# Two column halves for shift and scale at the start of a two-block transformer kernel, and half of three weight chunks ahead of the second

## The chip, the cores and the metric

The kernel runs on one core of one Trainium2 chip. The metric is the time of one execution on the device, in microseconds (us): the median of the runs. In the rows PE is TensorE (matrix multiply; PEld its weight load), DVE is VectorE, ACT is ScalarE, POOL is GpSimd, and SP only issues DMAs.

## What is computed

Two transformer blocks work on 256 tokens of width 2048, all in float32. The change is in the start of the first, up to its first output projection:

```python
silu_c = jax.nn.silu(c)
mod = silu_c @ w_ada[l] + b_ada[l]                    # w_ada: 2048 x 12288
shift_m, scale_m, gate_m, shift_f, scale_f, gate_f = jnp.split(mod, N_MOD, axis=-1)
h = modulate(rmsnorm(x, g_norm_mix[l]), shift_m, scale_m)   # normed * (1 + scale) + shift
proj = h @ w_in[l]                                    # w_in: 2048 x 3904
dq, dk, dv, q_lat, kv_lat, k_pe = jnp.split(proj, IN_SPLITS, axis=-1)
...                                                   # differential attention on dq, dk, dv
q = (rmsnorm(q_lat, g_q_a[l]) @ w_q_b[l]); kv = (rmsnorm(kv_lat, g_kv_a[l]) @ w_kv_b[l])
...                                                   # latent attention (MLA) on q, kv, k_pe
x = x + gate_m[:, None, :] * (jnp.concatenate([o_diff, o_mla], axis=-1) @ w_out[l])
```

`c` is one vector, so each of the six parts of `mod` is a vector of 2048. The rest of the first block (a 8192 wide feed-forward with its own shift, scale and gate) and the whole second block stay as they are.

## The kernel before

**Every weight passes a ring of four slots** (`RING`, `w_raw`), 1 MiB each. SP issues a load (line 399) when the slot's last user has released it. There are two kinds of load. A *weight load* holds four contraction tiles of 128 rows by 512 columns; ACT rounds it in two *halves* of 1024 columns to `w_hi` (L424), DVE subtracts to get `w_lo` (L429), and PE multiplies each half with 12 matmuls of 512 columns (L470: h_hi with w_hi, h_hi with w_lo, h_lo with w_hi; two contraction tiles, two token tiles). `w_hi` and `w_lo` also have four slots, one per half, so ACT can be at most four halves ahead of PE. A *chunk* is 512 output columns; with 16 contraction tiles it has 8 halves, and goes to one of two PSUM accumulators, `acc`.

An *ada load* holds 128 rows of one of the six parts of `w_ada`, 128x2048. DVE multiplies it with one value of silu(c) per row and adds it to `acc_ada` (L1575 for the first of 16, L1578 for the others; called a MAC below). After 16 of them the sum over the 128 partitions is taken by 16 matmuls against a column of ones (L2636, L2645 for the first scale; `ada_sum`) or, for a gate that is wanted in every row, by 4 matmuls of 512 columns (L2848, `gate_sum`), which ACT copies out (L1028).

**The start.** SP issues four ada loads, then x, then the other 28 of shift and scale. The parts come in the order `ADA_ORDER`: shift, scale, shift of the feed-forward, `gate_m`, scale of the feed-forward, last gate. When DVE has done all 32 MACs, PE sums the scale, DVE makes the factors (L1613, L1615), and piece by piece (two tiles of h of eight) ACT scales the transposed x (L772), DVE rounds (L1662) and subtracts (L1663), and PE starts on chunk 0.

**The chunks** of `w_in`, `w_q_b` and `w_kv_b` stand in `FIRST`, numbered 0 to 14. Halves are numbered through by g: chunk n of `w_in` has the halves 8n to 8n+7, g = 64 to 69 are `w_q_b`, 70 to 73 `w_kv_b`. `FIRST_MACS` says after which loads of a chunk an ada load follows. Everything else is hung on g by hand in `first_step`: copies of finished chunks (L884, L1803), rotary parts (L1766 to L1771), transposes (L494), latent norms. `HEAD_AT` says at which g each of the eight heads of the differential attention starts; a head is scores (L2771), a maximum (L1849), exponentials on ACT, the difference of the two softmaxes (L1861), a transpose, and the values (L2758). Heads 0 to 3 are normed by `head_scaled(0)` (L1838, L1841).

**After g = 73** come the transposes for the latent attention, and a loop over its eight heads (scores L2857 and L2858, maximum L1967, norm L1960, values L2876, copy L1973), with one MAC per turn on DVE (turn i is head i). In turns 0 and 1 PE and ACT also do the four gate sums. Then the output projection `w_out` starts: 4 chunks of 8 halves, 2 MACs each.

Engines run their own instructions in the order of the program and wait on semaphores; nothing is reordered.

## Time and profile before

| | us |
|---|---|
| median of 3 runs | 2719.41 |
| lowest and highest | 2716.62, 2720.58 |
| profiled execution | 2724.19 |
| its span, first to last instruction | 2722.5 |
| start of chunk 0 / 3 / 7 on PE in that span | 102.3 / 177.5 / 286.1 |
| start of `w_out` on PE | 415.8 |

A row of a timeline gives the start, the length, the engine and the line of an instruction; "x3" joins three in a row, and brackets tell how long the engine had been idle and what released it. The chain is the work that ended last, followed back from the end; each piece waited for the piece before it. Rows by stretch give busy time per engine, TensorE's granted clock (1.00 is full), and the share of their time in which the 16 DMA engines were busy, with what they moved.

### The profile page before, as it was taken

The page shows a single profiled execution, that of the slowest core. Times are in us where ns is not written, and L with a number is a line of the kernel's source. Part 1 is how long each engine was busy: PE and PEld are TensorE (multiplying, and loading weights), DVE is VectorE, ACT ScalarE, POOL GpSimd, SP SyncE. Part 2 cuts the span into 40 slices and gives each one's busy share as a digit, 9 for nine tenths or more (in the row PEclk, how much of TensorE's full clock was granted, in tenths as well). Part 3 has the DMA queues.
Part 4 walks back from the last instruction along what each step waited for, and adds up shares of the span by engine and source line. Part 5 has one row for each costly group of instructions (what it writes and reads, how often), then busy time and mean ns, then how long its engine had stood idle before and what let it go on. Part 6 is the DMA issues. An engine that isn't in the chain of part 4 may idle for free.

```text
span 2722.5 us, 30665 instructions
## 1 busy us (share of the span) xinstructions
PE 2594.5 (95%) x11981; PEld 2149.9 (79%) x11981; DVE 1637.6 (60%) x1806; ACT 1212.7 (45%) x1631; POOL 10.8 (0%) x62
## 2 busy tenths in 40 slices
PE   1699879999999999999999999999999999999999
PEld 1577767788888888888888888888888888888887
DVE  7888677777455555556555775556555554454554
ACT  1346444544433444444444664454444343344343
POOL 0000000000000000000000000000000000000000
PEclk9999899999999999999999999999999999999999
DMA  9898457687555556555554584345555555555554
GB/s 399 304 356 312 166 199 284 225 288 277 201 187 187 190 186 208 188 183 194 188 167 162 175 262 140 124 155 186 185 185 183 197 189 187 196 187 191 189 194 139
DMA packets 254815, 566.08 MB, mean 208 GB/s; under 512 B 9967, under 2 KB 25068, under 8 KB 242156
## 3 DMA queue, kind: packets, MB, share of 16 engines
q1 hardware_dynamic: 252164, 562.87, 60.1%
q10 hardware_dynamic: 2538, 1.65, 0.2%
q8 instruction: 77, 1.26, 0.2%
q14 instruction: 36, 0.29, 0.0%
HBM read 562.39 MB, written 2.10 MB: 207 GB/s over the span
## 4 chain that ended last, share of the span: by engine, by line
PE 88%; DVE 7%; DMA 3%; issue 1%; ACT 1%; ACTq 0%; DVEq 0%
PE acc L470 81%; DVE acc_ada L1578 3%; PE tp L494 3%; DVE w_lo L429 2%; DMA w_raw<-in_w_ada_dram 1%; DMA w_raw<-in_w_in_dram 1%; PE sc L3035 1%; PE sc L3127 0%; PE sc L3126 0%; ACT w_hi L424 0%; PE sc L3143 0%; PE sc L2645 0%; PE tp L2758 0%; DMA rowsA<-in_g_norm_mix_dram 0%; PE tp L2848 0%
## 5 line engine op out<-in xcount | busy, mean ns | idle before, releaser
L429 DVE TENSOR_TENSOR w_lo<-w_raw,w_hi 128x1024 fp32r<-128x1024 f32 (+2 forms) x878 | 1053.7, 1217 | 580.0 <-ACT w_hi L424 572.0
L424 ACT ACTIVATE w_hi<-w_raw 128x1024 fp32r<-128x1024 f32 (+2 forms) x878 | 913.0, 1055 | 868.9 <-PE acc L470 782.1
L470 PE MATMUL acc<-w_hi,h_hi 128*128 128x512 f32 (+2 forms) x2272 | 715.1, 396 | 5.2 <-DVE w_lo L429 4.0
L470 PE MATMUL acc<-w_lo,h_hi 128*128 128x512 f32 (+2 forms) x2272 | 701.5, 390 | 0.0
L470 PE MATMUL acc<-w_hi,h_lo 128*128 128x512 f32 (+2 forms) x2272 | 700.1, 389 | 0.0
L470 PEld LDWEIGHTS acc<-w_lo,h_hi 128*128 128x128 f32 x2272 | 428.9, 189 | 89.3
L470 PEld LDWEIGHTS acc<-w_hi,h_lo 128*128 128x128 f32 x2272 | 428.4, 189 | 89.0
L470 PEld LDWEIGHTS acc<-w_hi,h_hi 128*128 128x128 f32 x2272 | 418.5, 190 | 88.8 <-issue 7.5
L470 PE MATMUL acc<-w_hi,f_hi 128*128 128x512 f32 x864 | 268.7, 392 | 0.0
L470 PE MATMUL acc<-w_lo,f_hi 128*128 128x512 f32 x864 | 266.3, 389 | 0.0
L470 PE MATMUL acc<-w_hi,f_lo 128*128 128x512 f32 x864 | 265.9, 389 | 0.0
L1578 DVE SCALAR_TENSOR_TENSOR acc_ada<-w_raw,cT,acc_ada 128x2048 f32<-128x2048 f32 x92 | 216.0, 2348 | 12.0 <-DMA w_raw<-in_w_ada_dram 8.5
L470 PEld LDWEIGHTS acc<-w_lo,f_hi 128*128 128x128 f32 x864 | 162.2, 188 | 34.0
L470 PEld LDWEIGHTS acc<-w_hi,f_lo 128*128 128x128 f32 x864 | 162.2, 188 | 33.8
L470 PEld LDWEIGHTS acc<-w_hi,f_hi 128*128 128x128 f32 x864 | 161.5, 188 | 34.5 <-issue 1.2
L2017 DVE TENSOR_TENSOR relu<-relu 128x1024 f32<-128x1024 f32 x16 | 19.6, 1226 | 51.6 <-ACT relu L1076 51.6
L1076 ACT ACTIVATE relu<-acc 128x1024 f32<-128x1024 f32 x16 | 16.4, 1028 | 71.4 <-PE acc L470 71.4
L1748 DVE SCALAR_TENSOR_TENSOR h_lo<-tp,vecB,h_hi 128x256 fp32r<-128x256 f32 x32 | 14.0, 480 | 53.0 <-ACT h_hi L848 53.0
L2593 DVE SCALAR_TENSOR_TENSOR hs<-acc,stat,sg 128x512 f32<-128x512 f32 x22 | 15.5, 746 | 48.1 <-ACT sg L1492 48.1
L729 ACT ACTIVATE sc<-x_residual 128x512 f32<-128x512 f32 x40 | 23.6, 591 | 46.4 <-DVE x_residual L1995 21.0
L2569 DVE TENSOR_TENSOR f_lo<-tp,f_hi 128x512 f32 (+1 forms) x22 | 14.2, 686 | 48.5 <-ACT f_hi L1502 48.5
L494 PE MATMUL tp<-ident,rowsB 65*128 65x65 f32 x1 | 0.4, 370 | 44.8 <-DMA perow<-in_cmp_pe_v_dram 44.8
(425 smaller groups left out, 1688.9 us busy)
## 6 DMA issues: line engine op xcount, KB each, us to landing
w_raw<-in_w_ff_dram SPq DMA_DIRECT2D x128, 1024.0 KB, 5.3
w_raw<-in_w_in_dram SPq DMA_DIRECT2D x108, 1024.0 KB, 5.0
w_raw<-in_w_ada_dram SPq DMA_DIRECT2D x96, 1024.0 KB, 6.4
w_raw<-in_w_ffn_gate_dram SPq DMA_DIRECT2D x44, 1024.0 KB, 5.0
w_raw<-in_w_ffn_up_dram SPq DMA_DIRECT2D x44, 1024.0 KB, 5.0
w_raw<-in_w_ffn_down_dram SPq DMA_DIRECT2D x44, 1024.0 KB, 5.0
w_raw<-in_w_out_dram SPq DMA_DIRECT2D x32, 1024.0 KB, 5.0
w_raw<-in_w_up_fox_dram SPq DMA_DIRECT2D x8, 1024.0 KB, 5.0
```

Source lines behind the costliest of these rows:

```text
L424: nc.scalar.activation(dst, src, ACT.Copy).then_inc(hi_done, 1)
L429: nc.vector.tensor_tensor(dst, src, hi.bitcast(F32), ALU.subtract).then_inc(lo_done, 1)
L470: last = nc.tensor.matmul(acc[b][:, t, 0:width], st[:, kt, t * P:(t + 1) * P], w[:, slot, kt - 2 * j, 0:width], start=(kt == 0 and n == 0) ...
L494: last = nc.tensor.transpose(tp[b][dst], src, ident[0:k, 0:k])
L729: last = nc.scalar.activation(sc[t][:], x[:, t, c * CW:(c + 1) * CW], ACT.Square, accum_out=sums[:, k:k + 1])
L1076: nc.scalar.activation(relu[:], acc[a.slot(2)][:], ACT.Relu).then_inc(acc_free[a.slot(2)], 2)
L1578: V.scalar_tensor_tensor(a[:], w, c_k, a[:], ALU.mult, ALU.add).then_inc(S("mac_done"), 1)
L1748: last = V.scalar_tensor_tensor(h_lo[:, k, :], tp[u.slot(2)][:, kk * T:(kk + 1) * T], vecB[:, gain0 + k:gain0 + k + 1], h_hi[:, k, :].bitc ...
L2017: V.tensor_tensor(relu[:], relu[:], relu[:], ALU.mult).then_inc(S("relu_squared"), 1)
L2569: V.tensor_tensor(f2_lo[:, cols, :], tp[u.slot(2)][:].rearrange("p (a b) -> p a b", a=2), f2_hi[:, cols, :].bitcast(F32), ALU.subtract).th ...
L2593: V.scalar_tensor_tensor(hs2[:, t, :], acc[a.slot(2)][:, t, :], stat[:, 6 + t:7 + t], sg2[:, t, :], ALU.mult, ALU.mult).then_inc(acc_free[ ...
L3035: last = MM(dst, st, wk, start=q in (0, 6) and j == 0 and k == 0 and m == 0, stop=q in (5, 9) and j == 1 and k == 3 and m == 1)
```

## The change

- **Halves of columns.** Shift and scale are made in two stages of 1024 columns. An ada load now holds 1024 columns of shift and the same 1024 of scale for 128 rows, 128x2x1024 in rows of 4 KB in place of 8 KB. Stage 0 gives the first 8 tiles of h, stage 1 the last 8. x is loaded before all of them.
- **Rows on PE.** Five of the 16 loads of stage 0 (`ROW_TILES`) are multiplied on PE, 4 matmuls of 512 columns each with one column of silu(c) as the weights; the result is one row, which DVE adds to partition 0 (`row_sums`).
- **Half of the contraction ahead.** After stage 0 the first two loads of each of the chunks 0, 1, 2 go through, between the ada loads of stage 1 (`FRONT_W`, `FRONT_MACS`); then the last two of each. Chunk 2 goes to the two `sc` banks, since `acc` holds only two chunks.
- **MACs later.** The first three chunks lose their 10 MACs of later parts. Chunk 6 gets 4 (was 2), chunk 7 gets 3 (was 1), the attention loop 10 (was 8), each `w_out` chunk 3 (was 2). The four gate sums move from turns 0 and 1 of the attention loop to behind it.
- **Moved by hand:** heads 0 to 3 from g = 30, 33, 36, 39 to 36, 39, 42, 45; rotary parts of chunks 0 and 1 from g = 16, 22 to 26, 28, and their four transposes from 18, 19, 24, 25 to 28 to 31; the ones-sum of part 2 from g = 54 to 62; `head_scaled(0)` from 57 to 69; `mod_column(3)` from 57 to 66. The latent heads' outputs go to a buffer of their own (`oM`). `row_sums`, `front_mods` and so on are new functions for the start.

```diff
-FIRST_MACS = ((0, 2), (0, 1, 2, 3), (0, 1, 2, 3), (0, 1, 2, 3), (0, 1, 2, 3), (0, 1, 2, 3), (0, 2), (1,)) + 7 * ((0,),)
+FIRST_MACS = ((), (), (), (0, 1, 2, 3), (0, 1, 2, 3), (0, 1, 2, 3), (0, 1, 2, 3), (0, 1, 3)) + 7 * ((0,),)
 FIRST_TILES = {"w_in": KD, "w_q_b": 4, "w_kv_b": 2}
-HEAD_AT = (30, 33, 36, 39, 53, 56, 59, 62)
+FRONT_CHUNKS, STAGES = 3, 2
+ROW_TILES = (1, 4, 7, 10, 13)
+FRONT_W = ((0, 0), (0, 1), (1, 0), (1, 1), (2, 0), (2, 1), (0, 2), (0, 3), (1, 2), (1, 3), (2, 2), (2, 3))
+FRONT_MACS = ((0,), (1, 2, 3), (4, 5), (6, 7, 8), (9, 10, 11, 12, 13, 14), (15,))
+HEAD_AT = (36, 39, 42, 45, 53, 56, 59, 62)
...
+        mix_acc = place("mix_acc", [P, STAGES, D], F32, 0)
...
+        oM = place("oM", [P, HEADS, T], F32, 66)
...
+        front_load, at = {}, 0
+        for k in range(KD):
+            front_load["ada", 0, k] = at
+            at += 1
+        for i, piece in enumerate(FRONT_W):
+            front_load[piece] = at
+            at += 1
+            for k in FRONT_MACS[i] if i < len(FRONT_MACS) else ():
+                front_load["ada", 1, k] = at
+                at += 1
+
+        def mac_count(s, k):
+
+            return KD + k + 1 if s else k + 1 - sum(1 for r in ROW_TILES if r <= k)
...
-            ada_loads(RING)
             sp.dma_start(x[:], A["x"][0].rearrange("(t p) d -> p t d", p=P)).then_inc(S("x_loaded"), 16)
-            ada_loads(2 * KD - RING)
-            for nth in range(len(FIRST)):
-                if nth == 1:
+            for what, L in front_load.items():
+                if what[0] == "ada":
+                    _, s, k = what
+                    src = A["w_ada"][0][k * P:(k + 1) * P, 0:2 * D].rearrange("p (g n) -> p g n", g=2)
+                    freed = (S("row_macs"), ROW_TILES.index(k) + 1) if s == 0 and k in ROW_TILES else (mac_done, mac_count(s, k))
+                    ring(At(L), raw[:, At(L).slot(RING)].rearrange("p (g a) n -> p g (a n)", g=2),
+                         src[:, :, s * D // 2:(s + 1) * D // 2], freed[0], At(freed[1]))
+                else:
+                    nth, q = what
+                    name, col, width, nk = first_part(nth)
+                    src = A[name][0][CW * q:CW * (q + 1), col:col + width].rearrange("(k p) n -> p k n", p=P)
+                    ring(At(L), raw[:, At(L).slot(RING)], src, lo_done, At(2 * FRONT_W.index(what) + 2))
...
-            ada_loads(HEADS)
-            weights(A["w_out"][0], 4, KD, macs=2)
+            ada_loads(HEADS + 2)
+            weights(A["w_out"][0], 4, KD, macs=3, uniform=0)
...
+            front_hi(0, 0)
+            front_hi(0, 1)
+            for p in range(4):
+                front_piece(p)
+            for nth, q in FRONT_W[2:7]:
+                front_hi(nth, q)
+            front_piece(4)
+            front_piece(5)
+            front_hi(0, 3)
+            front_piece(6)
+            front_piece(7)
+            for nth, q in FRONT_W[8:]:
+                front_hi(nth, q)
...
-                if i < 2:
-                    for q in (2 * i, 2 * i + 1):
-                        gate_rows(gate_m, q)
-                    if i == 1:
-                        use += 4
-                if i >= 1:
...
+            for q in range(4):
+                gate_rows(gate_m, q)
+            use += 4
...
+            def row_sums():
+
+                dve.wait_ge(S("row_macs"), len(ROW_TILES))
+                dve.wait_ge(S("mac_done"), mac_count(0, KD - 1))
+                for c in range(4):
+                    to = mix_acc[0:1, 0, c * CW:(c + 1) * CW]
+                    last = V.tensor_tensor(to, to, acc[c // 2][0:1, c % 2, :], ALU.add)
+                last.then_inc(S("mac_done"), len(ROW_TILES))
...
+            row_sums()
+            front_lo(0, 0)
+            front_mac(1, 0)
+            front_mods(0)
+            front_lo(0, 1)
+            front_piece(0)
+            front_piece(1)
+            front_mac(1, 1)
+            front_mac(1, 2)
+            front_piece(2)
+            front_mac(1, 3)
+            front_piece(3)
+            for i in range(2, 6):
+                front_lo(*FRONT_W[i])
+                for k in FRONT_MACS[i]:
+                    front_mac(1, k)
+            front_lo(0, 2)
+            positions()
+            angles(0)
+            angles(1)
+            dve.sem_inc(S("angles_reduced"), 1)
+            front_mods(1)
+            front_piece(4)
+            front_piece(5)
+            front_lo(0, 3)
+            front_piece(6)
+            front_piece(7)
+            for nth, q in FRONT_W[8:]:
+                front_lo(nth, q)
...
-                    one_mac()
+                one_mac()
...
-            ada_sum(0, 2)
...
+            pe.wait_ge(S("mac_done"), 1)
+            for nth, k in enumerate(ROW_TILES):
+                L = At(front_load["ada", 0, k])
+                pe.wait_ge(raw_loaded[L.slot(RING)], L.round(RING).times(16).val(16))
+                for c in range(4):
+                    last = MM(acc[c // 2][0:1, c % 2, :], cT[:, k:k + 1], raw[:, L.slot(RING), c, :], start=nth == 0,
+                              stop=nth == len(ROW_TILES) - 1)
+                last.then_inc(S("row_macs"), 1)
...
+            front_turns(0)
+            for i, (nth, q) in enumerate(FRONT_W):
+                if i == 5:
+                    front_turns(1)
+                width = first_part(nth)[2]
+                for jj in range(2):
+                    j = 2 * q + jj
+                    pe.wait_ge(S("mix_ready"), j + 1)
+                    pe_half(pe, At(2 * i + jj), nth % 2, j, KD, width, h_hi, h_lo,
+                            [sc[t][:, 0:width] for t in range(NT)] if nth == FRONT_CHUNKS - 1 else None)
+                    if i in (0, 6):
+                        front_turn(j + 2)
+            pe.wait_ge(S("small_loaded"), 16 * SMALL)
+            TR(pe, At(11), [((slice(0, P), slice(0, NROWS)), rowsB[0:NROWS, :])])
+            use = 12
...
-                if i < 2:
-                    for q in (2 * i, 2 * i + 1):
-                        gate_sum(GATE_M, use, q)
-                    if i == 1:
-                        use += 4
...
+            for q in range(4):
+                gate_sum(GATE_M, use, q)
+            use += 4
```

DVE at the start of the program, before. `acc_ada` is where the MACs add, `w_lo` a weight half, `h_lo` a piece of h, `xs` the normed x:

```order
3 L1575 TENSOR_SCALAR acc_ada<-w_raw,cT 128x2048
4 L1578 SCALAR_TENSOR_TENSOR acc_ada<-w_raw,cT,acc_ada 128x2048 x15
5 L1575 TENSOR_SCALAR acc_ada<-w_raw,cT 128x2048
6 L1578 SCALAR_TENSOR_TENSOR acc_ada<-w_raw,cT,acc_ada 128x2048 x3
...
15 L1578 SCALAR_TENSOR_TENSOR acc_ada<-w_raw,cT,acc_ada 128x2048
16 L1592 TENSOR_TENSOR modT<-tp,vecA 128x16
17 L1578 SCALAR_TENSOR_TENSOR acc_ada<-w_raw,cT,acc_ada 128x2048 x8
18 L1613 TENSOR_TENSOR modT<-sc,vecA 128x4
19 L1615 SCALAR_TENSOR_TENSOR gmod<-modT,vecA 128x4
20 L429 TENSOR_TENSOR w_lo<-w_raw,w_hi 128x1024
```

And now, from the last MACs of stage 0 to the factors of stage 1 (`mix_acc` takes the place of `acc_ada`):

```order
9 L1679 SCALAR_TENSOR_TENSOR mix_acc<-w_raw,cT,mix_acc 128x2048 x4
10 L1687 TENSOR_TENSOR mix_acc<-mix_acc,acc 1x512 x4
11 L460 TENSOR_TENSOR w_lo<-w_raw,w_hi 128x1024 x2
12 L1676 TENSOR_SCALAR mix_acc<-w_raw,cT 128x2048
13 L1702 TENSOR_TENSOR modT<-tp,vecA 128x8
...
26 L460 TENSOR_TENSOR w_lo<-w_raw,w_hi 128x1024 x2
27 L1679 SCALAR_TENSOR_TENSOR mix_acc<-w_raw,cT,mix_acc 128x2048 x6
28 L460 TENSOR_TENSOR w_lo<-w_raw,w_hi 128x1024 x2
29 L1679 SCALAR_TENSOR_TENSOR mix_acc<-w_raw,cT,mix_acc 128x2048
30 L460 TENSOR_TENSOR w_lo<-w_raw,w_hi 128x1024 x2
31 L1748 CAST pos_f<-pos_i 128x2
```

Six weight loads now stand among the 16 MACs of stage 1, and the rotary angles (from row 31) stand ahead of the factors of stage 1 (row 48).

ACT at the end of the latent attention, before (`pmT` are transposed probabilities, `h_hi` rounded attention outputs, L424 the first halves of `w_out`):

```order
180 L1035 ACTIVATE pm,sums<-acc,mxs 128x256 x2
181 L1048 ACTIVATE pmT<-tp 128x512 x2
182 L424 ACTIVATE w_hi<-w_raw 128x1024 x2
183 L780 ACTIVATE h_hi<-oT 128x512
```

and now:

```order
179 L1107 ACTIVATE pm,sums<-acc,mxs 128x256 x2
180 L1115 ACTIVATE pmT<-tp 128x512 x2
181 L1100 ACTIVATE gate_m<-tp 128x512 x4
182 L455 ACTIVATE w_hi<-w_raw 128x1024 x2
183 L801 ACTIVATE h_hi<-oM 128x512
```

The four copies of the gate sums stand directly ahead of the first weight halves of `w_out`.

## Rows read from the trace of the kernel before

**Rows 1.** The page: busy time by engine; the chain by engine.
```profile
PE 2594.5 (95%) x11981; PEld 2149.9 (79%) x11981; DVE 1637.6 (60%) x1806; ACT 1212.7 (45%) x1631; POOL 10.8 (0%) x62
...
PE 88%; DVE 7%; DMA 3%; issue 1%; ACT 1%; ACTq 0%; DVEq 0%
```

**Rows 2.** Busy time by stretch; DMA share and GB/s stand last.
```profile
core 0: us, PE busy (x) PEld busy (x) DVE busy (x) ACT busy (x) POOL busy (x), PEclk, DMA share, GB/s
20.00:40.00 20.00, 0.00 (x0) 0.00 (x0) 15.96 (x7) 6.62 (x17) 0.00 (x0) 1.00 1.02 420
...
1200.00:1500.00 300.00, 299.08 (x1393) 249.00 (x1392) 167.91 (x211) 135.19 (x178) 0.00 (x0) 1.00 0.54 180
177.50:286.00 108.50, 107.66 (x529) 87.29 (x529) 89.48 (x107) 58.30 (x115) 0.00 (x0) 0.98 0.84 300
...
311.00:375.00 64.00, 47.19 (x225) 38.04 (x224) 46.07 (x65) 29.03 (x63) 0.00 (x0) 0.84 0.52 192
```

**Rows 3.** Timeline of DVE up to chunk 0: start, us, instruction, idle before.
```profile
22.64 2.35 DVE L1578 SCALAR_TENSOR_TENSOR acc_ada<-w_raw,cT,acc_ada 128x2048 f32<-128x2048 f32 x1 [5.06 <-DMA w_raw<-in_w_ada_dram]
...
46.19 7.26 DVE L1578 SCALAR_TENSOR_TENSOR acc_ada<-w_raw,cT,acc_ada 128x2048 f32<-128x2048 f32 x3 [0.37 <-DMA w_raw<-in_w_ada_dram]
53.47 1.28 DVE L1575 TENSOR_SCALAR acc_ada<-w_raw,cT 128x2048 f32<-128x2048 f32 x1
...
75.90 19.54 DVE L1578 SCALAR_TENSOR_TENSOR acc_ada<-w_raw,cT,acc_ada 128x2048 f32<-128x2048 f32 x8 [0.65 <-DVE modT L1592]
97.40 0.16 DVE L1613 TENSOR_TENSOR modT<-sc,vecA 128x4 f32<-128x4 f32 x1 [1.96 <-PE sc L2645]
...
99.51 0.69 DVE L1663 TENSOR_TENSOR h_lo<-ttmp,h_hi 128x512 fp32r<-128x512 f32 x1
...
105.82 2.34 DVE L429 TENSOR_TENSOR w_lo<-w_raw,w_hi 128x1024 fp32r<-128x1024 f32 x2
```

**Rows 4.** The chain at the start: start, us, engine and line.
```profile
51.10 2.35 DVE acc_ada L1578
...
95.49 6.99 PE sc L2645 x32
102.48 5.33 PE acc L470 x12
...
108.33 2.79 PE acc L470 x12
```

**Rows 5.** Timeline of ACT: one piece scaled, one weight half rounded.
```profile
97.85 1.02 ACT L772 ACTIVATE ttmp<-tp,modT,gmod 128x256 f32<-128x256 f32 x2 [1.34 <-DVEq L1617]
98.76 1.05 ACT L424 ACTIVATE w_hi<-w_raw 128x1024 fp32r<-128x1024 f32 x1
```

**Rows 6.** The gate sums' line on PE: ns min/median/max (two records each matmul).
```profile
L2848 PE MATMUL tp<-acc_ada,ones x16: 590/592/594, 376.1 to 725.0; 128*128 128x512 f32 x16
```

**Rows 7.** The loads' line on SP, first 120 us: issue to landing.
```profile
DMA to landing us min/median/max: 5.0/7.4/12.6
```

**Rows 8.** Timeline of PE: transposes after a pause; first matmuls of chunks 2, 3.
```profile
75.45 1.09 PE L494 MATMUL tp<-ident,xs 128*128 128x128 f32 x4 [4.67 <-DVEq L1593]
...
154.72 0.62 PE L470 MATMUL acc<-w_hi,h_hi 128*128 128x512 f32 x2
...
177.53 0.70 PE L470 MATMUL acc<-w_hi,h_hi 128*128 128x512 f32 x2
```

**Rows 9.** The chain between chunk 7 and the latent attention.
```profile
347.57 0.69 DVE proj L1803
348.26 2.26 DVE acc_ada L1578
...
353.09 2.18 issue
```

**Rows 10.** Timeline of DVE: heads 4 to 7 normed; the third maximum of the loop.
```profile
361.58 1.29 DVE L1841 TENSOR_TENSOR proj<-proj,rcp 128x512 f32<-128x512 f32 x2
...
384.50 0.69 DVE L1967 TENSOR_REDUCE mxs<-acc 128x2 f32<-128x512 f32 x1 [1.10 <-PE acc L2858]
```

**Rows 11.** The chain at the end of the latent attention.
```profile
376.25 1.72 PE tp L2848 x4
...
409.88 0.63 DVE pm L1960 x2
410.55 0.66 PE tp L494 x4
411.20 2.88 PE sc L2876 x8
414.14 0.30 issue
414.44 1.23 DVE w_lo L429
415.81 9.25 PE acc L470 x27
```

**Rows 12.** Timeline of ACT: two of the four copies of the gate sums.
```profile
377.93 1.08 ACT L1028 ACTIVATE gate_m<-tp 128x512 f32<-128x512 f32 x2
```

400 lines of the change are left out of this document (216 added, 184 removed).

## The prediction

> **What bounds the kernel now.** First the page: TensorE is busy for 95% of the span, and the chain lies on it for 88% [rows 1]. So nearly everywhere only less work for TensorE would shorten the kernel, and the change takes no matmul away; it can gain only where TensorE stands idle. The stretches show where. From 20 to 40 us it does nothing at all, while DMA is full (share 1.02) [rows 2]; DVE's timeline and the chain go on like that to 95.5 us, first MACs that wait for loads, then MACs back to back [rows 3, 4]. The second idle place is between chunk 7 and the output projection: 47.2 us busy of 64 from 311 to 375 [rows 2]. In between (177.5 to 286.0, chunks 3 to 6) TensorE is busy 107.7 of 108.5 us, DVE 89.5, DMA 84% [rows 2].
>
> I take the working in two parts: when chunk 3 starts (before: 177.5 [rows 8]), and what the way from there to `w_out` costs more or less. Behind that, TensorE has work without gaps; a third MAC per `w_out` chunk adds 2.4 us of DVE to chunks of 22 us in which DVE has some 7 us to spare, and I count it at nothing; if that room were gone, it would cost 2.4 us for each of 4 chunks.
>
> **Stage 0.** Before, the 16th MAC begins at 51.10 and ends at 53.5 [rows 4], behind x and 16 loads; nine loads took 46.19 - 22.64, 2.62 us each, with DMA full [rows 3, 2]. The new order brings the same bytes, so 53.5 is where I start. Two things delay it.
> The rows are now 4 KB long. No row shows that. With rows of 8 KB the stretch gives 420/1.02 = 412 GB/s of a full DMA share, with the 2 KB rows of the feed-forward weights 180/0.54 = 333 [rows 2]: 2.55 and 3.15 us for 1 MiB. If a DMA row has a fixed cost, 4 KB lies a third of the way up: 2.75, or 16 x 0.20 = 3.2 us (ends 0 and 9.6).
> The five loads on PE: a 512 column float32 matmul takes 1.72/2 = 0.86 us [rows 11], two records each [rows 6]. After a pause TensorE works at 1.2 GHz: the sums take 6.99 us and the first half 5.33 against 2.79 later [rows 4], four transposes 1.09 after 4.67 us of pause [rows 8]. So a load takes 3.4 to 6.9 us there, where a MAC takes 2.4. At the longer time the slot comes free so late that, with 5.0 us from issue to landing [rows 7], DMA idles 1.4 us (6.9 + 5.0 against four loads of 2.62); five times gives 0 to 7. The engine gets warm during such a row, so I take 0.8 in all. The last MAC of stage 0 then ends at 53.5 + 3.2 + 0.8 = 57.5.
> The rule of the Trainium skill that speaks against my 3.2 is in "DMA: Bandwidth & Descriptors", Specifications: line rate needs at least 512 B. By it 4 KB would cost nothing over 8 KB, and both stages would end earlier, the sum by about 4 us. The trace does not bear it out as it stands, since the 2 KB stretch gives 333 and not 412 GB/s for a full share.
>
> **Stage 1.** From 57.5 the path is: four additions of one row, 2.6 (the nearest row is an h_lo of 512 columns, 0.69 with 0.1 overlapped [rows 3]); 16 sums by TensorE out of a pause, 7.0 [rows 4]; the factors, three operations as L1613 at 0.16 with gaps [rows 3], 0.8. That is 68.0. From here DVE has a list without a hole: w_lo of the second load 2.3, four pieces 2.6, 15 MACs at 19.54/8 = 2.44 make 36.7, w_lo of four loads 9.3 (2.34 each) [rows 3], together 50.9. It also waits: for the first pieces (ACT 1.02 and about 0.6 more) [rows 5], and for w_hi halves that ACT can't make until TensorE has freed a slot. 2.5 us, ends 0 and 6. The last MAC ends at 121.4. DMA by itself: 22 loads, 16 x 2.75 + 6 x 3.15 = 62.9 behind 55.1, plus the MAC: 120.4. Two engines are thus equally late here, and neither can be speeded up alone. TensorE meanwhile does ten halves, 28 us at full clock, 53 at half, in 51: it comes through, warm or in part cold.
> At 121.4 the sums again find TensorE out of a pause (it had nothing since the fifth weight load): 7.2. The rotary angles on DVE (4.6) lie beside them. Factors 0.8, a transpose that needs the bank they free 1.1, and TensorE starts the 11th half at 130.8, the first at low clock. 14 halves at 2.74 ((177.53 - 154.72 - 0.9)/8 [rows 8]) make 38.4, the low clock 2.5 (5.33 - 2.79), two transposes 1.0: **chunk 3 starts at 172.7**, 4.8 us earlier than 177.5. Its 33 us of matmuls ahead are worth so little since the last MAC, which ended at 95.5, now ends at 121.4, and is followed by 14 halves instead of 24 with their own MACs between.
>
> **From chunk 3 to w_out.** (a) Two transposes that stood in chunk 2 come into chunk 3: +0.9. (b) In chunks 3 to 6 DVE gets 2 more MACs (4.9), two rotary parts and lambda (4.3): 98.7 us of work in about 103 (the ones-sum has left for chunk 7), where it had 89.5 in 108.5 [rows 2]. Its lead of up to four halves hides most; +1.0, ends 0 and 4. (c) Chunk 7: the ones-sum comes in with its own cold matmuls behind it, which only moves 6 us; two more MACs, 4.9 us of DVE, of which the chunk has 7 us idle: +1.0, ends 0 and 4. (d) `head_scaled(0)`, 1.3 us for its two products [rows 10] and 0.4 of small ones, moves out of chunk 7 to g = 69, where the chain is DVE [rows 9]; with `mod_column` +1.9, ends 1 and 2.5. (e) The latent loop: without gate sums in the first two turns, the third maximum does not wait 1.10 us [rows 10], and the MAC that only writes (L1575, 1.28 [rows 3]) falls into a turn that DVE bounds: -1.9. At the end DVE's two extra MACs go into the pauses for the last values. But TensorE does four gate matmuls, 3.4 us or 6.9 cold [rows 11], and **ACT stands in order**: the last gate copy (0.54 [rows 12]) must be done before the first w_hi of `w_out` (1.05), then w_lo (1.2). From the end of the values, 414.1 - 1.9, that is 412.2 + 3.4 + 0.6 + 1.05 + 1.2 = 418.5, or 422.0 cold, where it was 415.8 [rows 11]: +2.7 to +6.2, I take +4.2. Before, the w_hi was made under the values.
> Sum: 0.9 + 1.0 + 1.0 + 1.9 + 4.2 = +9.0, against -4.8: **+4.2**. The profiled execution (2724.2, span 2722.5) would become 2728.4; it lies 4.8 above the median of the runs, so the median goes from 2719.4 to 2723.6. Differences under about 0.2% (5.4 us) can't be told from none in a measurement of this kernel.
>
> **Rivals.** (1) **Faster**: DMA takes 4 KB rows like 8 KB, no slot is held up, DVE waits for nothing. Stage 0 ends at 53.5, the last MAC at 53.5 + 10.5 + 50.9 = 114.9, chunk 3 starts at 166.2: -11.3. With (b), (c) at nothing, (d) 1, (e) 2.7: +4.6, together -6.7, 2713; with the sums at full clock too (3.5 twice) 2706. For it: DVE took its MACs without a hole from 75.9 to 95.4 [rows 3]. This takes in the skill's rule on row lengths. I name it 2711. (2) **Slower, the ring**: a weight load holds its slot until ACT and DVE are through with it, and ACT waits for TensorE's w_hi slots at low clock; so both bounds of stage 1 add up instead of lying beside each other. It decides as soon as the holes of stage 1 exceed 6 us: last MAC at 127, chunk 3 at 178.4, +0.9 + 9.0 = 2729. For it: issue to landing of 7.4 in the median [rows 7], nearly the whole turn of a ring of four. Against: in the same rows DVE kept 2.44 a load. (3) **Slower, the way behind**: the start gains 4.8, but (b), (c), (d) and (e) stand at their upper ends, 0.9 + 4 + 4 + 2.5 + 6.2 = 17.6: 2732. (4) That TensorE doesn't start ahead at all: only if the first pieces of h waited for stage 1, and the order of DVE's rows excludes it; no chance of its own.
>
> **Chances.** Forecast 0.36, from 2714 to 2724.8, within 0.2%; faster (1) 0.27; slower (2) 0.27 and (3) 0.10. So faster 0.27, same 0.36, slower 0.37. The signs are nearly balanced, since a gain of 5 to 11 stands against a loss of 5 to 12 at other places. The range takes in most of (1) and of (2) and (3): 2709 to 2732. The forecast's own range is 2716 to 2729.
>
> **What will show it.** Five groups of four row matmuls on TensorE, 3.4 to 6.9 us each; last MAC of stage 0 near 57.5, of stage 1 near 121; a pause of TensorE before each ones-sum and 7 us for each; chunk 3 at 172.7; between stage ends DMA share near 1; `w_out` starting 5 to 8 us behind the last values instead of 1.7. I am wrong if chunk 3 starts before 168 or after 177, or if ACT's gate copies end without TensorE waiting.

## The result and the profile after

| | before | after |
|---|---|---|
| median, us | 2719.41 | 2728.50 |
| lowest and highest | 2716.62, 2725.27 | 2723.52, 2735.17 |
| runs | 11 | 11 |
| profiled execution (span) | 2724.19 (2722.5) | 2728.53 (2726.6) |

The changed kernel is slower: ratio 1.0029, 95% interval 1.0021 to 1.0037, or 7.9 us (5.7 to 10.1). The range held it (2709 to 2732). The likeliest case, 2723.6 and within 0.2% of before, did not come: it was 0.29%, the slower side.

Again first the page of the changed kernel, the engines and the chain by engine; [rows 1] are the same lines of before.

```profile
PE 2625.1 (96%) x12021; PEld 2159.9 (79%) x12021; DVE 1620.8 (59%) x1794; ACT 1221.5 (45%) x1643; POOL 10.8 (0%) x62
...
PE 92%; DVE 4%; DMA 2%; ACT 1%; issue 1%; SPq 0%; DVEq 0%; ACTq 0%
```

TensorE is busy 31 us longer: the row matmuls (24.0 us in five groups), and more matmuls at low clock. By stretch, as [rows 2] (columns: busy us and instructions of PE, PEld, DVE, ACT, POOL, then the clock, DMA share, GB/s):

```profile
core 0: us, PE busy (x) PEld busy (x) DVE busy (x) ACT busy (x) POOL busy (x), PEclk, DMA share, GB/s
20.00:40.00 20.00, 9.13 (x18) 1.30 (x16) 9.01 (x7) 1.49 (x2) 0.00 (x0) 0.83 0.93 351
177.50:286.00 108.50, 108.20 (x546) 88.45 (x544) 97.94 (x126) 62.26 (x127) 0.00 (x0) 1.00 0.89 320
311.00:375.00 64.00, 45.11 (x217) 36.19 (x215) 44.82 (x66) 26.87 (x57) 0.00 (x0) 0.84 0.49 180
```

From 20 to 40 us the DMA share is 0.93, where it was 1.02: the loads no longer come without a gap. From 177.5 to 286 DVE is busy 97.9 us where it was 89.5, and from 311 to 375 TensorE does even less than before. DVE's timeline answers to [rows 3]; "x4" with L1687 is `row_sums`:

```profile
28.32 2.35 DVE L1679 SCALAR_TENSOR_TENSOR mix_acc<-w_raw,cT,mix_acc 128x2048 f32<-128x2048 f32 x1 [7.07 <-DMA w_raw<-in_w_ada_dram]
...
37.00 4.80 DVE L1679 SCALAR_TENSOR_TENSOR mix_acc<-w_raw,cT,mix_acc 128x2048 f32<-128x2048 f32 x2 [3.79 <-DMA w_raw<-in_w_ada_dram]
...
54.77 2.35 DVE L1679 SCALAR_TENSOR_TENSOR mix_acc<-w_raw,cT,mix_acc 128x2048 f32<-128x2048 f32 x1 [0.35 <-DMA w_raw<-in_w_ada_dram]
57.23 2.47 DVE L1687 TENSOR_TENSOR mix_acc<-mix_acc,acc 1x512 f32<-1x512 f32 x4
...
120.37 2.35 DVE L1679 SCALAR_TENSOR_TENSOR mix_acc<-w_raw,cT,mix_acc 128x2048 f32<-128x2048 f32 x1
```

The MACs wait 7.07 and 3.79 us for loads; the last of stage 0 ends at 57.1, the last of stage 1 at 122.7. The timeline of TensorE, as [rows 8], shows the same from the other side, and what follows:

```profile
33.87 5.08 PE L2839 MATMUL acc<-w_raw,cT 128*1 128x512 f32 x8 [8.54 <-DMA w_raw<-in_w_ada_dram]
...
59.75 6.99 PE L2851 MATMUL tp<-ones,mix_acc 128*128 128x1 f32 x32 [5.17 <-DVE mix_acc L1687]
...
122.86 6.96 PE L2851 MATMUL tp<-ones,mix_acc 128*128 128x1 f32 x32 [14.10 <-DVE mix_acc L1679]
...
173.28 1.06 PE L510 MATMUL acc<-w_hi,h_hi 128*128 128x512 f32 x2 [1.78 <-DVE w_lo L460]
...
335.55 2.05 PE L2902 MATMUL tp<-proj,pdT 128*128 128x128 f32 x8 [6.33 <-DVE c_lo L1946]
```

Both ones-sums stand behind a pause and take 7 us. Chunk 3 starts at 173.28, 4.2 us earlier than before. At 335.55 the values wait 6.33 us for the last `c_lo`. Before it was 4.90:

```profile
334.19 2.04 PE L2758 MATMUL tp<-proj,pdT 128*128 128x128 f32 x8 [4.90 <-DVE c_lo L1823]
```

The chain at the end of the latent attention, against [rows 11]:

```profile
410.48 1.82 PE sc L3013 x8
412.30 3.54 PE tp L2990 x8
...
416.36 1.06 ACT w_hi L455
417.44 1.24 DVE w_lo L460
418.81 21.34 PE acc L510 x86
```

`w_out` starts at 418.81 in place of 415.81. Behind that, hardly anything is left that the change made. The offset between the two traces is 1.72 us at the first gate product behind `w_out`, 2.79 at the first relu of the feed-forward part, the same 2.79 at the places behind it up to 1546 us, and 4.04 from 1668 us on. Each step is a stretch at low clock that is longer in one trace than in the other, with the same instructions and pauses. At the start of the feed-forward part before has

```profile
515.24 1.22 PE L470 MATMUL acc<-w_hi,h_hi 128*128 128x512 f32 x2
516.26 1.05 PE L470 MATMUL acc<-w_lo,h_hi 128*128 128x512 f32 x2
517.11 0.79 PE L470 MATMUL acc<-w_hi,h_lo 128*128 128x512 f32 x2
```

and after

```profile
516.97 1.22 PE L510 MATMUL acc<-w_hi,h_hi 128*128 128x512 f32 x2
...
520.55 1.05 PE L510 MATMUL acc<-w_lo,h_hi 128*128 128x512 f32 x2
521.40 0.71 PE L510 MATMUL acc<-w_hi,h_lo 128*128 128x512 f32 x2
```

A pair of records is 1.05 us at 1.2 GHz and 0.62 at 2.4. After has five pairs of the low kind (two of them stand in the gap) where before has two, though both began the same way.

### The profile page after: what moved, and what is told of

It reads as the page before. It is cut to its first block, busy times and chain, and to the rows that moved or that the text cites. A ratio compares the mean times of both kernels' runs of the same rounds, so it can differ in the third digit from the quotient of the medians.

```text
span 2726.6 us, 30768 instructions
## 1 busy us (share of the span) xinstructions
PE 2625.1 (96%) x12021; PEld 2159.9 (79%) x12021; DVE 1620.8 (59%) x1794; ACT 1221.5 (45%) x1643; POOL 10.8 (0%) x62
## 4 chain that ended last, share of the span: by engine, by line
PE 92%; DVE 4%; DMA 2%; ACT 1%; issue 1%; SPq 0%; DVEq 0%; ACTq 0%
PE acc L510 83%; PE tp L534 3%; DMA w_raw<-in_w_ada_dram 2%; DVE acc_ada L1648 1%; DVE w_lo L460 1%; DVE mix_acc L1679 1%; PE sc L3175 1%; PE sc L510 1%; DMA w_raw<-in_w_in_dram 1%; PE tp L2851 1%; PE sc L3267 0%; PE sc L3266 0%; PE sc L2917 0%; PE sc L3283 0%; PE tp L2902 0%
## 5 line engine op out<-in xcount | busy, mean ns | idle before, releaser
L510 PE MATMUL acc<-w_hi,h_hi 128*128 128x512 f32 (+2 forms) x2240 | 705.0, 396 | 8.1 <-DVE w_lo L460 5.9
L510 PE MATMUL acc<-w_lo,h_hi 128*128 128x512 f32 (+2 forms) x2240 | 691.9, 390 | 0.0
L510 PE MATMUL acc<-w_hi,h_lo 128*128 128x512 f32 (+2 forms) x2240 | 690.4, 390 | 0.0
L510 PEld LDWEIGHTS acc<-w_lo,h_hi 128*128 128x128 f32 x2240 | 423.4, 189 | 87.9
L510 PEld LDWEIGHTS acc<-w_hi,h_lo 128*128 128x128 f32 x2240 | 422.6, 189 | 87.5
L510 PEld LDWEIGHTS acc<-w_hi,h_hi 128*128 128x128 f32 x2240 | 413.0, 190 | 91.3 <-issue 11.8
L1648 DVE SCALAR_TENSOR_TENSOR acc_ada<-w_raw,cT,acc_ada 128x2048 f32<-128x2048 f32 x62 | 145.5, 2346 | 1.1 <-DVE proj L1991 1.1
L1679 DVE SCALAR_TENSOR_TENSOR mix_acc<-w_raw,cT,mix_acc 128x2048 f32<-128x2048 f32 x25 | 58.8, 2350 | 21.6 <-DMA w_raw<-in_w_ada_dram 20.6
L2839 PE MATMUL acc<-w_raw,cT 128*1 128x512 f32 x40 | 24.0, 758 | 22.6 <-DMA w_raw<-in_w_ada_dram 22.6
```

The lines of the kernel that those rows point to most:

```text
L510: last = nc.tensor.matmul(banks[t], st[:, kt, t * P:(t + 1) * P], w[:, slot, kt - 2 * j, 0:width], start=(kt == 0 and n == 0), stop=(kt == ...
L1648: V.scalar_tensor_tensor(a[:], w, c_k, a[:], ALU.mult, ALU.add).then_inc(S("mac_done"), 1)
L1679: V.scalar_tensor_tensor(to, w, cT[:, k:k + 1], to, ALU.mult, ALU.add).then_inc(S("mac_done"), 1)
L2839: last = MM(acc[c // 2][0:1, c % 2, :], cT[:, k:k + 1], raw[:, L.slot(RING), c, :], start=nth == 0, stop=nth == len(ROW_TILES) - 1)
```

## The experiments

All ratios are to the kernel before; times of starts are from one profiled execution of each.

**The kernels once more.** Nothing is edited here; these two were run again for their traces.

> The kernel before, unchanged, profiled a second time. Theory (how fast the first loads land differs from execution to execution, with all behind it fixed): the 16th MAC ends 0.5 to 2.5 us off 53.45 and chunk 3 starts off 177.53 by less, and TensorE's clock at the start of w_out and of the feed-forward part rises at another instant, with up to 3 us in it. Rival (the first profile is exact): every start within 0.3 us.

Ratio 0.9999 (0.9990 to 1.0009), and yet a span of 2714.3 us in place of 2722.5. The 16th MAC ended at 54.1 instead of 53.5 and chunk 3 started at 178.0 (2.8 us ahead of its first transposes, as in the first trace) instead of 177.5. Then it got ahead:

```profile
411.24 0.70 PE L470 MATMUL acc<-w_hi,h_hi 128*128 128x512 f32 x2 [1.74 <-DVE w_lo L429]
```

`w_out` starts 4.6 us earlier than in the first trace. The row of the stretch from 280 to 430 us, first of the first trace, then of this one, says why:

```profile
280.00:430.00 150.00, 119.62 (x581) 97.12 (x581) 114.09 (x168) 68.03 (x154) 1.81 (x1) 0.87 0.55 196
```

```profile
280.00:430.00 150.00, 120.00 (x607) 97.45 (x608) 117.52 (x171) 71.21 (x156) 1.80 (x1) 0.93 0.59 209
```

120 us of TensorE at a mean clock of 0.87 lose 15.6 us to the low clock, at 0.93 only 8.4. (Busy time times what the clock lacks to 1.00.) The same product, added up in stretches of 10 us over the whole span, gives 21.4 us for the first trace and 12.9 for the second, and the spans are 8.2 us apart. The prediction had read its rows behind 286 us from an execution with more low clock. The theory is right in kind, but the effect is larger than it allowed: 4.6 us at `w_out`, not up to 3.

> The changed kernel, unchanged, profiled a second time. Theory (the rows of this kernel that repeat are fixed by its order, and the part that differs is the landing of the first loads and the instants at which TensorE's clock changes): the last MAC of stage 0 ends at 57 to 59.5, chunk 3 starts at 173 to 175.5, w_out 242 to 246 us behind it. Rival (the difference of 7.9 us is all order): chunk 3 and w_out start within 0.3 us of 173.28 and 418.81.

Ratio 1.0027 (1.0017 to 1.0037). The last MAC of stage 0 ended at 59.8, 2.7 us later than in the first trace, and

```profile
176.40 0.70 PE L510 MATMUL acc<-w_hi,h_hi 128*128 128x512 f32 x2 [1.78 <-DVE w_lo L460]
```

chunk 3 starts at 176.40 and `w_out` at 421.65, 245.3 us behind it (245.5 in the first trace). With the three variants below that keep this start there are five traces: chunk 3 at 173.3, 173.8, 175.0, 175.3, 176.4, on average 174.8. The first trace was the earliest of the five. The rival is out; the theory holds in kind, though 59.8 and 176.40 lie 0.3 and 0.9 us outside its limits.

**Rows on TensorE.** `ROW_TILES` empty, `row_sums` gone:

```diff
-ROW_TILES = (1, 4, 7, 10, 13)
+ROW_TILES = ()
...
-            row_sums()
```

> The changed kernel with all 16 loads of stage 0 as MACs on DVE, none as rows on TensorE, and so without the four additions of row_sums (2.47 us). Theory (stage 0 is bound by DMA, so the row matmuls take nothing off the path and only add row_sums): the last MAC of stage 0 ends within 0.8 us of 57.1, the ones-sum starts at 57.0 to 57.8 in place of 59.75, and chunk 3 starts 1 to 2.5 us earlier than 173.28. Rival A (DVE would be late with 16 MACs at 2.35 us): the last MAC ends at 58.5 or later, and nothing is won. Rival B (the row matmuls held ring slots and cost DMA time): the last MAC ends at 55.5 or earlier, the first MACs without pauses, and chunk 3 starts 3.5 us or more earlier.

Ratio 1.0016 (1.0007 to 1.0024), 3.5 us less than the changed kernel. Both ratios have intervals of about 2 us to either side, so a difference between two of them is known to about 3 us; that holds for each such difference below. The last MAC of stage 0:

```profile
50.63 4.84 DVE L1679 SCALAR_TENSOR_TENSOR mix_acc<-w_raw,cT,mix_acc 128x2048 f32<-128x2048 f32 x2 [0.16 <-DMA w_raw<-in_w_ada_dram]
...
55.62 6.96 PE L2850 MATMUL tp<-ones,mix_acc 128*128 128x1 f32 x32 [47.34 <-DVE mix_acc L1679]
```

The last MAC ends at 55.5, the ones-sum starts 4.1 us earlier, chunk 3 at 170.40, 2.9 earlier. My theory was wrong in its first half: the row matmuls did take something off the path. The DMA share from 20 to 30 us, first of the changed kernel, then of this one:

```profile
20.00:30.00 10.00, 4.05 (x10) 0.59 (x8) 2.94 (x2) 1.28 (x1) 0.00 (x0) 1.00 0.83 288
```

```profile
20.00:30.00 10.00, 0.00 (x0) 0.00 (x0) 7.33 (x6) 1.13 (x1) 0.00 (x0) 1.00 0.97 357
```

With rows 288 GB/s, without 357. The slot that is held can be followed: the MAC that waits 7.07 us at 28.32 is that of load 5, which goes to the slot of load 1, and load 1 was in the row matmuls of 13.98 to 20.46. Without rows its MAC ended at 16.28, and no MAC of the stage behind the first waits more than 1.4 us. Rival B is right in kind, though chunk 3 gained less than its 3.5 us; over all traces the last MAC of stage 0 ends at 57.1 to 59.8 with rows (five) and at 55.5 to 57.1 without (five), 2.2 us apart on average, and `row_sums` comes on top.

**Rows of 4 KB.** The kernel before with the shape of its first 32 loads changed:

```diff
-                src = A["w_ada"][0][bass.ds(k.times(P).val(), P), group * D:(group + 1) * D]
+                src = A["w_ada"][0][m.k % KD * P:(m.k % KD + 1) * P, 0:2 * D].rearrange("p (g n) -> p g n", g=2)
+                src = src[:, :, s * D // 2:(s + 1) * D // 2]
```

> The kernel before with only the shape of its first 32 loads changed: 128 rows of 2 x 1024 columns in pieces of 4 KB, where it had rows of 8 KB; order, bytes, MACs and everything else as before (the shift and scale are then made of other columns, so its values differ from the reference). Theory (4 KB pieces cost 0.2 us for each load of 1 MiB): the last MAC of the 32 ends 6.4 us (5 to 8) later than 95.5, chunk 0 starts near 108.7 in place of 102.3, and the time rises by 5 to 7.5 us. Rival (the length of the pieces does not matter from 512 B up): all of these within 1 us of before.

The last eight MACs begin at 80.63, before at 75.90 [rows 3], and chunk 3 4.8 us later:

```profile
80.63 19.54 DVE L1584 SCALAR_TENSOR_TENSOR acc_ada<-w_raw,cT,acc_ada 128x2048 f32<-128x2048 f32 x8 [0.64 <-DVE modT L1598]
...
182.28 0.70 PE L470 MATMUL acc<-w_hi,h_hi 128*128 128x512 f32 x2 [0.94 <-DVE w_lo L429]
```

The 16th MAC ended 3.1 us later (56.6), 0.5 of it since the first began later. So a load costs 0.13 to 0.19 us more; for 16 loads that is 2.6 to 3.1 us where the theory had 3.2, and for 32 it was 4.7 where it had 6.4, short of its range. The same share of DMA moved less, from 30 to 40 us 403 GB/s at 1.03 in this kernel against 422 at 1.02 in the kernel before. "DMA: Bandwidth & Descriptors" of the Trainium skill (Specifications) gives 512 B as the least transfer for line rate. This trace does not bear out that everything above is the same. But the ratio is 1.0003 (0.9995 to 1.0012), 0.8 us. `w_out` was 4.0 us later than in the first trace of before, and that although the low clock took less from 280 to 430 us:

```profile
280.00:430.00 150.00, 119.91 (x607) 97.87 (x604) 112.72 (x170) 71.81 (x164) 1.80 (x1) 0.91 0.55 191
```

That is 10.8 us by this row, against 15.6 and 8.4 in the two traces of before. The interval of the time ends at 3.3 us, below the 4.7. The clock was a little better than before in the mean of all executions, 0.9918 against 0.9911; over the 2594.5 us in which TensorE is busy that is 1.8 us, an estimate. How much of a delay of 4.7 us at the start is left at the end is not settled.

**Warm before the second ones-sum.** Ten unused matmuls at once, and the angles moved:

```diff
+                    for _ in range(10):
+                        MM(tp[b][:], ones[:], mix_acc[:, 0, 0:CW], start=True, stop=True)
                 pe.wait_ge(S("mac_done"), KD * (s + 1))
...
-            positions()
-            angles(0)
-            angles(1)
-            dve.sem_inc(S("angles_reduced"), 1)
             front_mods(1)
```

> The changed kernel with ten 512 column matmuls whose result is not used, on TensorE ahead of the second ones-sum (in its pause of 14.1 us), and with the rotary angles (4.6 us on DVE) moved from ahead of front_mods(1) to behind the last w_lo of the front. Theory (the second ones-sum pays the low clock, 6.96 us for 32 records): it takes 3.5 to 4 us, the half behind it starts at 127 to 128 in place of 131.31 and is at full clock, and chunk 3 starts 4 to 6 us earlier than 173.28. Rival A (what follows stage 1 is bound by loads or by ACT and DVE, not by TensorE): the sum is shorter but chunk 3 moves by less than 2 us. Rival B (the extra matmuls run at the low clock throughout and end behind the last MAC): the sum starts later than 122.86 and nothing is won.

Ratio 1.0033 (1.0020 to 1.0046), from five executions: nothing won. The unused matmuls were through at 119.5, long before the last MAC, and the clock had fallen again:

```profile
124.25 6.89 PE L2853 MATMUL tp<-ones,mix_acc 128*128 128x1 f32 x32 [4.78 <-DVE mix_acc L1679]
```

4.78 us of pause, 6.89 us of sum. So neither the theory nor the rivals were tested, and the last two runs with unused matmuls, further down, do it again. What is left of this run is the other edit alone: with the angles out of the way DVE takes the factors 7.0 us behind the last MAC, in the changed kernel 7.4.

**The gate sums.** In turns 6, 7 and 8 instead of behind the loop, on PE and ACT:

```diff
+GATE_TURNS = {6: (0,), 7: (1,), 8: (2, 3)}
...
+                for q in GATE_TURNS.get(i, ()):
+                    gate_rows(gate_m, q, gate_use(q))
...
-            for q in range(4):
-                gate_rows(gate_m, q)
```

> The changed kernel, but the four gate sums and their copies stand in turns 6, 7 and 8 of the latent loop (one, one, two) instead of behind it. Theory (the gate copies stand ahead of the first w_hi of the output projection on ACT): the first w_hi goes back beside the last values, and w_out starts at 414.5 to 415.5 in place of 418.81, 3 to 4.5 us earlier; the time falls by 3 to 4. Rival (the start of w_out is bound by its loads, or by DVE's two extra MACs at the end of the loop): w_out starts at 418 or later and the time stays within 1 us.

Ratio 1.0017 (1.0008 to 1.0026), 3.3 us less. This execution started late (chunk 3 at 175.31), so `w_out` is to be counted from the start of the loop's first scores: 41.0 us, where it was 43.7 in the changed kernel and 41.5 before. The wait ahead of it:

```profile
418.23 1.19 PE L524 MATMUL acc<-w_hi,h_hi 128*128 128x512 f32 x2 [3.83 <-DVE w_lo L474]
```

The first w_hi is no longer held up, and that gives 2.6 us, a little under the theory's range. But TensorE now waits 3.83 us here, before it was 1.74. The chain shows for what:

```profile
411.77 2.26 DVE acc_ada L1661
...
414.28 2.34 DVE acc_ada L1661
...
416.87 1.23 DVE w_lo L474
```

These are DVE's two extra MACs at the end of the loop, the second half of the rival. The prediction had put them into pauses. They are hidden only while the gate sums take longer; once those are gone, they set the start of `w_out`.

**The norm of heads 0 to 3.** It goes behind the `c_lo` of g = 70, and `mod_column(3)` from g = 66 to 65:

```diff
-                    if g == 69:
-                        head_scaled(0)
...
                     latent_lo(24, 4, "g_kv_a", 3)
+                    head_scaled(0)
```

> The changed kernel with head_scaled(0) (1.44 us on DVE) behind the c_lo of g = 70 instead of ahead of it at g = 69, and mod_column(3) at g = 65 in place of 66. Theory (the norm stands in DVE's chain to c_lo, on which TensorE waits 6.33 us at the last values): that wait falls to 4.7 to 5.1, and w_out starts 1.0 to 1.6 us earlier, counted from chunk 3's start (245.5 us in the changed kernel, so 243.9 to 244.5); the norm fits into DVE's 2.2 us of waiting behind c_lo. Rival (DVE is full from there to the latent loop, so the work only moves): the wait shrinks, but w_out keeps its 245.5 within 0.5.

Ratio 1.0022 (1.0012 to 1.0033), 1.9 us less.

```profile
330.59 2.05 PE L2902 MATMUL tp<-proj,pdT 128*128 128x128 f32 x8 [4.89 <-DVE c_lo L1946]
...
413.37 1.19 PE L510 MATMUL acc<-w_hi,h_hi 128*128 128x512 f32 x2 [2.98 <-DVE w_lo L460]
```

The wait falls from 6.33 to 4.89, as the theory says, and the wait of 0.79 us for `mod_column(3)` is gone. `w_out` comes 239.5 us behind chunk 3 (173.83), over 4 us less than the theory had: from 280 to 430 us the low clock took 9.0 us here, in stretches of 10 us, and 13.7 in the first trace of the changed kernel. In the time the gain is not shown, since 1.9 us is less than the 3 us to which the difference is known.

**Only the later part, on the kernel before.** Start and heads as before; the MACs, the gate sums, part 2's ones-sum and `head_scaled(0)` as in the change:

```diff
-FIRST_MACS = ((0, 2), (0, 1, 2, 3), (0, 1, 2, 3), (0, 1, 2, 3), (0, 1, 2, 3), (0, 1, 2, 3), (0, 2), (1,)) + 7 * ((0,),)
+FIRST_MACS = ((), (), (), (0, 1, 2, 3), (0, 1, 2, 3), (0, 1, 2, 3), (0, 1, 2, 3), (0, 1, 3)) + 7 * ((0,),)
...
-            ada_loads(HEADS)
-            weights(A["w_out"][0], 4, KD, macs=2)
+            ada_loads(HEADS + 2)
+            weights(A["w_out"][0], 4, KD, macs=3, uniform=0)
```

> The kernel before with only the later part of the change: its start and its heads stay, but the MACs of chunks 0 to 2 (10) go to chunk 6 (4), chunk 7 (3), the latent loop (10) and w_out (3 per chunk), the gate sums stand behind the loop, the ones-sum of part 2 at g = 62 and head_scaled(0) at g = 69. Theory (the loss lies behind chunk 3): chunk 3 starts at 174.5 to 177.5 (two pauses of 1.0 and 1.2 us for w_lo go), from there to w_out it takes 241.5 to 246 us in place of 233.2 and 238.3 in the two profiles of the kernel before, and the ratio is 1.001 to 1.003. Rival (the later part is nearly free, and the changed start is what costs): w_out within 239 us of chunk 3, and a ratio under 1.0005.

Ratio 1.0013 (1.0005 to 1.0022): 3.5 us (1.4 to 6.0) of the 7.9. Chunk 3 starts at 175.0 (the transposes behind its first half stand at 177.79, where they stood at 180.35), and `w_out`, 240.8 us behind it, at

```profile
415.78 1.19 PE L471 MATMUL acc<-w_hi,h_hi 128*128 128x512 f32 x2 [2.98 <-DVE w_lo L430]
```

This is the most telling run, though it has one trace. With the ten MACs gone from chunks 0 to 2, the **old** start reaches chunk 3 2.8 us earlier too, as early as the new one does on average (174.8, from 173.3 to 176.4). So, as far as one trace tells, the new start with its 33 us of matmuls ahead gained nothing of its own at chunk 3. The way from there to `w_out` is 4.6 us longer with the new start (245.4 against 240.8), or 3.5 if the two variants with the same code behind chunk 3 are counted in (without rows 244.0, warm and angles 242.5). The time of this run has a second reading. Its mean clock over all executions was 0.9896, before 0.9911, which is 3.9 us more of low clock by the same estimate, as much as its whole loss. The estimate counts pauses too, so it is an upper one. Of the 6.3 us that the later part costs (3.5, and the 2.8 gained ahead of chunk 3), up to 3.9 can be low clock behind its pauses, and the rest is the pauses themselves.

Without the rows the new start reached chunk 3 at 170.4 and 173.8 in two traces, 2.9 us on average ahead of this run.

**Eight MACs back.** No rows, gate sums in turns, the norm later, and eight MACs between the weight loads behind stage 1:

```diff
+LATE_MACS = {7: (32, 33), 8: (34,), 9: (35, 36), 10: (37,), 11: (38, 39)}
```

> The changed kernel with four edits: no row matmuls; gate sums in turns 6 to 8; head_scaled(0) and mod_column(3) as in the run before; and eight MACs of the later parts between the weight loads behind stage 1, so that chunk 7, the latent loop and w_out have as many as in the kernel before (1, 8 and 2 per chunk). Theory (the start gains, and what the change lost behind it lay in work that had been moved there): chunk 3 starts at 168 to 172 (the eight MACs fit beside 14 halves of TensorE), from there to w_out it takes 237 to 240 us where the changed kernel takes 245.5 and the kernel before 238.3, and the time is 2712 to 2717, 4 to 8 us below the kernel before. Rival (the eight MACs hold the halves up, since DVE has 34 us of work there and DMA 47): chunk 3 starts at 174 or later, and the time is 2718 or above.

Ratio 1.0001 (0.9993 to 1.0010), median 2720.9. The rival: chunk 3 starts at 177.25, and the halves wait for w_lo:

```profile
151.20 0.70 PE L528 MATMUL acc<-w_hi,h_hi 128*128 128x512 f32 x2 [1.86 <-DVE w_lo L478]
...
164.05 0.70 PE L528 MATMUL sc<-w_hi,h_hi 128*128 128x512 f32 x2 [1.68 <-DVE w_lo L478]
...
177.25 0.70 PE L528 MATMUL acc<-w_hi,h_hi 128*128 128x512 f32 x2 [2.00 <-DVE w_lo L478]
```

At 151.20 that is DVE, which had two MACs in a row ahead of this w_lo. Behind that w_lo itself waits for w_hi, and w_hi for its load. ACT, and then two stretches with the DMA share next to last:

```profile
161.59 2.00 ACT L473 ACTIVATE w_hi<-w_raw 128x1024 fp32r<-128x1024 f32 x2 [6.96 <-DMA w_raw<-in_w_in_dram]
...
131.00:141.00 10.00, 10.00 (x42) 8.10 (x42) 3.83 (x4) 4.34 (x7) 0.00 (x1) 0.87 0.08 13
...
151.00:161.00 10.00, 9.80 (x43) 8.14 (x44) 9.90 (x7) 2.01 (x2) 0.00 (x0) 1.00 1.02 392
```

ACT waits 5.2, 7.0, 3.0 and 6.2 us for the loads of the four w_hi that stand between 152 and 176 us; in the changed kernel it waits there for TensorE. I had seen a DMA share of 0.53 from 120 to 180 us of the changed kernel and taken it for room. But the idle time lies at the start, where the four slots hold loads that wait for TensorE (share 0.08), and from 151 us on DMA is full (1.02 and 1.03). A weight load and two ada loads are 7.9 us of DMA at the 2.62 us of [rows 3] and 7.3 us of DVE, where two halves of TensorE take 5.5.

> The kernel of the run before with sixteen 512 column matmuls whose result is not used on TensorE ahead of the second ones-sum: two after each of the MACs 10 to 14 of stage 1, and six after MAC 15, so that no pause over about 1 us is left. Theory (the low clock comes from the pause of 14 us): the ones-sum takes 3.5 to 4.2 us in place of 6.96, the halves behind it run at full clock, and chunk 3 starts 3.5 to 5.5 us earlier than in the run before. Rival A (TensorE's path there is hidden behind DVE's angles, 4.6 us, and the factors): the ones-sum is shorter, but chunk 3 gains 0 to 2 us. Rival B (the extra matmuls run at the low clock and end late): the ones-sum starts over 1 us later and nothing is won.

Ratio 1.0012 (1.0003 to 1.0020), nothing won.

```profile
119.19 3.96 PE L2877 MATMUL tp<-ones,mix_acc 128*128 128x1 f32 x32
126.97 1.08 PE L552 MATMUL tp<-ident,xs 128*128 128x128 f32 x4 [2.88 <-DVEq L1723]
```

The ones-sum takes 3.96 us, but DVE is not ready: its angles end at 126.4, and the factors follow at 126.53, 7.4 us behind the last MAC as in the changed kernel. TensorE waits 2.88 us there, and its clock has fallen by then. Rival A. Chunk 3 starts at 178.19, 0.9 us later than in the run before; that place is also held by the loads that the run before showed, so it could not have shown a gain.

**Three edits, without the eight MACs; and then warm and angles.** Both edits stand above; the unused matmuls now come two after each of the MACs 10 to 14 and six after MAC 15:

```diff
+                    for m, count in ((10, 2), (11, 2), (12, 2), (13, 2), (14, 2), (15, 6)):
+                        pe.wait_ge(S("mac_done"), KD + m)
+                        for _ in range(count):
+                            MM(tp[b][:], ones[:], mix_acc[:, 0, 0:CW], start=True, stop=True)
```

> The changed kernel with three edits together and no others: no row matmuls, gate sums in turns 6 to 8, head_scaled(0) and mod_column(3) as in the run that moved the norm. Theory (each was worth what it gave alone, 3.5, 3.3 and 1.9 us by the ratios, and they lie at three places of one path): the ratio to the kernel before falls from 1.0029 to 0.999 to 1.0005, chunk 3 starts at 170 to 172.5 and w_out 236.5 to 240 us behind it. Rival (the gains overlap, since the ring behind chunk 3 is bound by DMA and catches up with the start): the start gains, but from chunk 3 to w_out it takes 241 us or more and the ratio stays at 1.001 or above.

Ratio 0.9988 (0.9980 to 0.9997), median 2718.0: 3.3 us faster than the kernel before (0.8 to 5.4) and 11.2 faster than the changed kernel. The three had given 8.7 together, which is the same within what is known of each. Chunk 3 at 173.82 (later than expected, the last MAC of stage 0 was at 56.8), `w_out` at 412.10, 238.3 behind it.

> The kernel of the run before with the sixteen unused matmuls ahead of the second ones-sum (two after each of the MACs 10 to 14, six after MAC 15) and the rotary angles behind the last w_lo of the front. Theory (ones-sum at the low clock and DVE's angles lie side by side, so that one edit alone gives nothing, and both together do): the ones-sum takes 3.5 to 4.2 us, the half behind it starts 3 to 4 us earlier and at full clock, and chunk 3 starts 3 to 5 us earlier than in the run before, at 166 to 169. Rival (ACT, DVE and the loads behind stage 1 set when the halves can run): the half behind the sum is earlier, but chunk 3 gains under 1.5 us.

Ratio 0.9973 (0.9964 to 0.9983), median 2714.17: 7.3 us faster than the kernel before, and 3.8 by the medians than the run before.

```profile
120.58 4.80 PE L2867 MATMUL tp<-ones,mix_acc 128*128 128x1 f32 x32 [0.47 <-DVE mix_acc L1692]
...
169.70 0.70 PE L524 MATMUL acc<-w_hi,h_hi 128*128 128x512 f32 x2 [1.78 <-DVE w_lo L474]
...
407.60 1.19 PE L524 MATMUL acc<-w_hi,h_hi 128*128 128x512 f32 x2 [3.84 <-DVE w_lo L474]
```

The pause is 0.47 us and the sum 4.80, more than expected. TensorE's clock fell inside the sum, with the engine busy all the time (the clock stands third from the end):

```profile
122.00:123.00 1.00, 1.00 (x11) 1.00 (x10) 1.00 (x2) 0.00 (x0) 0.00 (x0) 1.00 1.06 412
123.00:124.00 1.00, 1.00 (x7) 1.00 (x7) 0.37 (x1) 0.00 (x0) 0.00 (x0) 0.51 1.05 408
```

It came back near 130 us, so the half behind the sum started 3.7 us earlier, as expected, but not at full clock. DVE takes the factors at 125.42, 4.9 us behind the last MAC; in the run before it was 7.4 (129.34). Chunk 3 is 4.1 us earlier than in the run before, later than the expected 166 to 169. Of the 4.1 us, 2.5 lie between the last MAC and the factors, and 1.4 ahead of them, where the last MAC of stage 1 ended at 120.5 in place of 121.9; why it did is not shown. Sum at low clock and angles were two nearly equal paths side by side. From the last MAC to the factors the warm sum alone gave nothing (7.4, in the kernel with eight MACs back), the angles alone 0.4 (7.0, in the run "Warm before the second ones-sum"), and both 2.5.

## Why the prediction was off

**Right.** Stage 0 at 57.5 (57.1; 59.8 in the second trace), ones-sums of 7.0 us behind pauses, the half behind the second at 130.8 (131.31), 14 halves in 41.9 us (41.97), chunk 3 at 172.7 (173.28), `w_out` starting at 418.5 to 422 (418.81, 421.65) and behind it no difference of order. Against the one trace of before, the sum +4.2 was met to 0.1: 2728.5 against 2728.4. The median of 2728.5 lies in the range of 2709 to 2732, and at the edge of the forecast's own range (2716 to 2729). One sum is off: the terms behind the last MAC (121.4, 7.2, 0.8, 1.1) make 130.5, not 130.8.

**The row matmuls, term of 0.8 us.** It was 2.2. I had computed that a slot comes free late only if a row takes 6.9 us; rows took 3.6 to 6.5, and the first of them, 6.48, already left DVE waiting 7.07 us. DMA's share fell to 0.83 and 0.72 (second trace) between 20 and 30 us. The range of the term, 0 to 7, had it. The other term of stage 0, 3.2 for the rows of 4 KB, was near: 2.6 to 3.1. With rows, stage 0 ended at 58.6 on average of five traces, 1.1 later than forecast.

**Stage 1, 61.3 us from the ones-sum to the last MAC.** 63.0, 63.4 in the second trace, and 63.1 without rows; 62.1 to 65.0 over the ten traces with this order. The term that was too small is DVE's waiting, 2.5: in the first trace it waited 5.2 us between the factors and the last MAC, 2.9 for `w_hi` halves, 2.1 for pieces of h and 0.2 for loads.

**The term of the start, -4.8.** By five traces of the new start and two of the old it is -3.0 (174.8 against 177.8). What I had put down to the new start belonged to the ten MACs that left chunks 0 to 2: the old start without them gains the same 2.8, in its one trace. The step that failed is the one that gives the 33 us of matmuls ahead a small worth because the last MAC now ends at 121.4: I compared with the kernel before, where I ought to have compared with the kernel before without those MACs. Then the worth is nothing, within the 1 to 2 us by which such traces differ.

**(d), the norm: +1.9.** The wait at the values grew by 1.43 us (6.33 against 4.90), and TensorE waited 0.79 for `mod_column(3)`: 2.2 in all. Moving both back took both waits away; the 1.9 us in the time are too few to be told from none.

**(e), +4.2 and -1.9.** From the loop's first scores to `w_out` it was +2.1 and +1.5 in the two traces against the first and second of before, for my +4.2, in which the -1.9 is already counted. So the term was 2.4 too large. The loop up to the end of the values became 2.7 us shorter (3.3 between the second traces), not 1.9, and from there to `w_out` it took 6.5 us in both traces of the changed kernel, 1.7 before: I had taken a time between gate sums at full clock (6.3) and at low clock (9.8), and they ran at full clock (3.54 and 3.55). That ACT's copies stand ahead of `w_hi` is shown by the chain (412.30 to 416.36) and by the 2.6 us that came back. That DVE's two extra MACs go into pauses is true only beside the gate sums, as the run that moved these shows.

**(a) to (c), and w_out's third MAC.** From chunk 3 to q_b I had +2.9; it was +2.8 between the first traces and +6.4 between the second, most of the difference being clock. The third MAC cost nothing: TensorE has no wait of over 0.6 us between 419 and 510 us.

**The sum.** From chunk 3 to `w_out` the changed kernel took 245.4 us on average of two traces, before 235.8: +9.6 for my +9.0. That is no confirmation of the terms: up to the loop's first scores it was +5.1 between the first traces and +10.5 between the second, for my +4.8, and behind them +2.1 and +1.5 for my +4.2. With -3.0 for the start the sum is +6.6, inside the 5.7 to 10.1 of the ratio. The same code took from 233.3 to 238.3 us on this way before and from 242.5 to 245.5 after, so what is left of the 3.7 us by which the sum was off can't be divided further. That I met the one trace of after to 0.1 us was luck: its start was the earliest of five, before's rows behind 286 us had 7 us more of low clock than its second trace, and the terms (a) to (d) and (e) were off in opposite directions.

**The rivals.** (1) did not come, (4) neither. (2) has the right mechanism, slots that are held, at another place and size: in stage 0, and the last MAC of stage 1 at 122.7 and 125.9, not 127. (3) has the right sign, but (a) to (e) stood at +9.6, not +17.6. "Slower" came as a sum of small excesses, which no rival described; its chance, 0.37, held it.

## What to carry to other kernels

Work that is put ahead of a bound has to be priced against the old order with the same load: take the displaced work out of the old kernel first, and see whether anything is left to gain. Where two paths of nearly equal length end together (a sum at low clock and 4.6 us on another engine), an edit of either shows little (0 and 0.4 us here), and only both together tell (2.5). Ask also what stands next in line once a wait is taken away: behind the gate copies stood two MACs. When a tenth of a per cent matters, take the trace of the kernel before twice, since a difference between two single traces of up to 8 us was in the clock alone.

## What the runs showed of the hardware

- TensorE's clock moved the same kernel by 8.2 us (spans 2722.5 and 2714.3), at the places behind pauses: over all runs the same instructions between 1500 and 1800 us lost from 3.4 to 6.9 us to it (summed over stretches of 10 us). "TensorE: Matmul & The Clock Gate" of the Trainium skill (Part 1) says that the cold stretch differs from run to run of one kernel; these traces agree, and 0.3% of the span is as large as the effect studied.
- Unused matmuls kept the clock at 1.00 up to the sum only where they reached up to it: after 4.78 us of pause the sum was as slow as after 14.10 (6.89 and 6.96 us), after 0.47 us it took 4.80, and directly behind them 3.96. Even then the clock did not last. It fell to half inside the sum of one-column matmuls, near 123 us in the last run, with TensorE busy since the pause of 0.47 us, and the matmuls behind ran at the low level until near 130.
- A mean DMA share of 0.53 was no free room. The idle part lay where the ring was full of loads that waited for TensorE (share 0.08 from 131 to 141 us with the eight MACs back), and behind it DMA was full (1.02 from 151 to 161 us) and ACT waited up to 7.0 us for a load.
